# Two hybrid blocks on one core: the router on rows that are not yet normalised, the w_ada products in pairs, the attention's filling spread, and the order of the last experts

## The chip, the cores and the metric

The kernel runs on one core of one Trainium2 chip. The metric is device microseconds of one execution; the time before is 1055.93 us, the median of three runs (1053.69 to 1056.76).

## The reference, cut to what matters

256 rows of width 1024, float32, go through two blocks.

The first block: `h = rms_norm(x, g_mix)`, a projection by `w_in`, two attentions (8 causal heads with a forget gate, then 4 differential heads), gates, `w_o` and the residual. Then a mixture of experts:

```python
h = rms_norm(x, g_moe)
gl = h @ w_group + b_group            # 4 groups; the best one is taken
el = (h @ w_expert)[group] + b_expert # 8 experts of that group
ep = softmax(el); vals, idx = top_k(ep, 2); vals = vals / sum(vals)
weight = softmax(gl)[group] * vals
out[token] += weight * ((silu(h @ w1[e]) * (h @ w3[e])) @ w2[e])
x = rms_norm(x + out, g_final)
```

There are 32 experts; each has 6 MiB of weights (w1, w3: 1024x512, w2: 512x1024), all of which are read. The second block has `mod = silu(c) @ w_ada + b_ada` (w_ada is 1024x3072, 12 MiB, and depends on nothing computed before it), a projection by 1024x10240 weights, block attention, a short convolution, gates and output products.

## The kernel before, in words

Every engine runs a list of its own, in its order; semaphores join them. `O1.steps` (first block up to w_o) and `O2.steps` (second block) are lists of steps written out by a planner, and each engine's program walks them and does its share of each step.

**Weights.** SP loads chunks of 2 MiB in the order of the list `chunks` (line 831 issues each, the `dma_start` itself is L830). A chunk goes to a slot of a ring of five; the experts use three (areas 5, 6 and 7) besides, so eight chunks can be on their way or waiting. Four of six `ada` chunks stand behind `wo1` in the list; of those, the first has an area of its own (slot 8). SP waits in order: a chunk is issued when the one before it in its slot is used up (`released`). The first expert chunks wait for `s_y` 4 (the input of w_o is complete), the one in area 7 for the end of w_o.

**Products.** The dense products run on fp32r pairs: ACT copies a quarter chunk to its rounded high part (L1835), DVE or POOL subtracts to get the low part (L1253, L2187), and PE makes three products. All `matmul` calls go through L778. The experts use plain float32 weights.

**The attention's filling.** From the projections dq on, the dense products are handed out by a generator, `fill_first`: in each of 18 iterations of the attention loop, `next(fill)` is called twice (for i below 16), and puts one quarter chunk (or one w_ada product) between the small steps of a head: scores (`qk`), bias (`bf`), softmax (`soft` on DVE and ACT), transposes (`p_turn`, L965), P times V. The generator has 30 pieces, five are taken ahead of the loop; what is left at i = 16 is run then. `pa`, `pb` (the outputs of both attentions times w_pa, w_pb), then `wo0`, `wo1` follow.

**w_ada.** `ada_pe(i)`: eight products of a 32-column stationary (silu(c), divided by 32, in each column) with 512 columns of w_ada, into four groups of 32 partitions; ACT copies the bank to ACC; `ada_sum_pe(i)` adds the partitions by four one-column products with a column of ones. i = 0, 1 are run in the filling, i = 2 to 5 in the router.

**The router** (`route_pe` and `route` of each engine), after `wo1`: sum of squares per row on ACT (rows 0 to 127) and DVE (the others), rsqrt on POOL (L2175), scaled rows XS in the order of the experts' weights, 16 transposes (L959), 8 copies that multiply by g_moe, 8 products with the routing weights `wr`, transposes back, bias; then a chain of small DVE operations: softmax over groups, best group, softmax over its 8 experts, the two best, a table of selected experts SS. PE counts ranks by prefix sums (`cnt`), DVE builds PmR, the 0/1 matrix that selects the rows of four experts at a time (64 slots for each). XShR and XSlR are the high and low part of XS.

**The experts** (`experts_pe`). Per expert e: half a of w1, w3 (a chunk) times the gathered rows xe, `down(e-1)` (w2 of the expert before), every second time `scatter` (two experts added back to their rows, with PTR, into four accumulating banks), half b, two `gather` steps for the group of four that comes next (row selection by PmR, evicted by DVE with the factor g_moe), and two transposes of the activation Hb (L1202). ACT does Silu (L2011), copies y out (L1990) and makes its high part with the expert's weight as factor (L2000); DVE multiplies, evicts, and makes the low part. For e >= 28 DVE also makes four diagonals (L1256), PE spreads them over the partitions (8 matmul records) and DVE copies the result (L1622), as `spread`. At k = 1 of each four, PE multiplies PmR with the weights W32, which gives the weight of each slot. After the last expert each engine tests whether an expert has more than 64 rows (`flag`), which these inputs don't give; PE does so behind the last scatter, then runs five warm-up products, and goes on to the second block, whose first work on PE is `turn3` (transposes, L959).

## Time and profile before

| | us |
|---|---|
| median of 3 runs | 1055.93 |
| profiled execution, its time | 1055.72 |
| profiled execution, its span | 1053.9 |
| PE busy | 989.2 (94%) |
| DVE, ACT, POOL busy | 393.3, 368.7, 125.2 |
| moved by DMA | 307.92 MB |

The span starts with the first instruction and ends with the last; the time of an execution holds 1.8 us more than the span. "PE" is the matrix engine's products, "PEld" its weight loads, "SPq" the queue on which SP issues DMAs. The clock column is the granted clock of PE as a share of full speed: 1.00 is 2.4 GHz, 0.50 is 1.2 GHz. A busy PE is one with a product under way, whatever its clock.

### The profile page before, as it was taken

What the parts mean: (1) busy time and instruction counts of PE and PEld (TensorE: products, weight loads), DVE (VectorE), ACT (ScalarE), POOL (GpSimd) and SP (SyncE); (2) the same over time, 40 slices, a digit from 0 to 9 for tenths busy, and PEclk for the clock granted to TensorE, in tenths of its full rate; (3) what the DMA queues carried; (4) which work ended last, traced back from release to release, by engine and by line L of the source; (5) the groups of instructions that cost most, each with busy time, mean ns of one, the idle gap of its engine ahead of it and who ended that gap; (6) DMA issues with size and microseconds to landing.
All of it is one profiled execution on the core that took longest, in us unless ns stands there. A gap on an engine that the chain in (4) does not pass through costs nothing.

```text
span 1053.9 us, 14601 instructions
## 1 busy us (share of the span) xinstructions
PE 989.2 (94%) x6197; PEld 690.7 (66%) x6197; DVE 393.3 (37%) x761; ACT 368.7 (35%) x606; POOL 125.2 (12%) x79
## 2 busy tenths in 40 slices
PE   7999997999999999999999898876999999999996
PEld 6888886965434443443333333336999999999994
DVE  4454446845111111121211111125334444774464
ACT  4546664541111111111111111115445555554443
POOL 1111020120000000000000000001321111351122
PEclk9999998998999999999999999996999999999998
DMA  8973644697999999999999999995555545445300
GB/s 277 382 263 143 239 162 161 225 421 300 412 420 419 420 419 419 419 419 420 419 420 419 420 419 420 418 401 215 179 212 187 187 141 187 161 160 195 145 2 40
DMA packets 84043, 307.92 MB, mean 292 GB/s; under 512 B 6623, under 2 KB 13176, under 8 KB 59392
## 3 DMA queue, kind: packets, MB, share of 16 engines
q1 hardware_dynamic: 80184, 302.16, 73.2%
q10 hardware_dynamic: 3784, 4.73, 1.4%
q8 instruction: 51, 0.84, 0.3%
q14 instruction: 24, 0.20, 0.1%
HBM read 305.81 MB, written 2.63 MB: 293 GB/s over the span
## 4 chain that ended last, share of the span: by engine, by line
PE 65%; SPq 17%; DVE 8%; ACT 4%; DMA 3%; issue 2%; POOL 1%; POOLq 0%; ACTq 0%; DVEq 0%
PE bank L778 63%; SPq L830 17%; DMA ring<-in_w 3%; DVE arena L1253 2%; DVE arena L1256 2%; DVE wR L1253 2%; DVE arena L1259 1%; ACT wR L1835 1%; PE bank L1202 1%; ACT arena L2011 1%; PE bank L965 1%; POOL small L2175 1%; POOL wR L2187 0%; DMA arena<-in_x 0%; PE bank L959 0%
## 5 line engine op out<-in xcount | busy, mean ns | idle before, releaser
L778 PE MATMUL bank<-hTR,wR 128*128 128x256 f32 x2520 | 316.2, 286 | 5.6 <-DVE hTR L1253 2.3
L778 PEld LDWEIGHTS bank<-hTR,wR 128*128 128x128 f32 x2520 | 307.9, 193 | 10.0 <-issue 5.1
L778 PE MATMUL bank<-ring,arena 128*64 128x512 f32 (+1 forms) x1040 | 224.8, 596 | 8.9 <-DMA ring<-in_w 8.0
L1835 ACT ACTIVATE wR<-ring 128x1024 fp32r<-128x1024 f32 x161 | 168.3, 1054 | 109.8 <-PE bank L778 108.0
L1253 DVE TENSOR_TENSOR wR<-ring,wR 128x1024 fp32r<-128x1024 f32 x125 | 155.3, 1247 | 136.1 <-ACT wR L1835 135.7
L778 PE MATMUL bank<-arena 128*64 128x512 f32 (+8 forms) x794 | 169.0, 535 | 6.3 <-DMA arena<-in_w 3.4
L778 PEld LDWEIGHTS bank<-ring,arena 128*64 128x64 f32 (+1 forms) x1040 | 68.7, 135 | 141.3 <-issue 128.8
L1253 DVE TENSOR_TENSOR arena<-arena,bank 128x256 f32<-128x256 f32 (+1 forms) x36 | 16.1, 450 | 349.1 <-ACT arena L2011 347.4
L1990 ACT ACTIVATE arena<-bank 64x512 f32<-64x512 f32 x64 | 37.9, 593 | 288.7 <-PE bank L778 288.4
L2187 POOL TENSOR_TENSOR wR<-ring,wR 128x1024 fp32r<-128x1024 f32 x36 | 87.9, 2440 | 331.3 <-ACT wR L1835 331.3
L778 PEld LDWEIGHTS bank<-arena 128*64 128x64 f32 (+5 forms) x794 | 65.2, 149 | 90.8 <-issue 83.4
L2175 POOL TENSOR_TENSOR small<-small,mhalf 128x1 f32<-128x1 f32 (+1 forms) x12 | 9.0, 756 | 490.4 <-DVE small L1259 482.9
L2011 ACT ACTIVATE arena<-bank 128x256 f32<-128x256 f32 x32 | 12.3, 384 | 106.5 <-PE bank L778 106.5
L778 PE MATMUL bank<-wR,hTR 128*128 128x512 f32 x192 | 45.3, 393 | 0.0
L778 PEld LDWEIGHTS bank<-PmR,XShR 128*128 128x128 f32 x128 | 25.1, 196 | 24.5 <-issue 23.5
L778 PEld LDWEIGHTS bank<-wR,hTR 128*128 128x128 f32 x192 | 35.6, 188 | 8.3 <-issue 1.0
L778 PE MATMUL bank<-PmR,XShR 128*128 128x256 f32 x128 | 36.4, 315 | 0.7 <-DVE small L1436 0.6
L778 PE MATMUL bank<-PmR,XSlR 128*128 128x256 f32 x128 | 33.0, 289 | 0.0
L1256 DVE TENSOR_SCALAR arena<-bank,col 128x256 f32<-128x256 f32 x68 | 30.0, 478 | 6.5 <-PE bank L778 5.7
L1253 DVE TENSOR_TENSOR arena<-bank,arena 128x512 f32<-128x512 f32 (+2 forms) x30 | 19.6, 665 | 19.3 <-PE bank L778 17.0
L778 PEld LDWEIGHTS bank<-PmR,XSlR 128*128 128x128 f32 x128 | 25.3, 198 | 0.0
L1253 DVE TENSOR_TENSOR arena<-arena 128x512 f32<-128x512 f32 (+7 forms) x38 | 21.2, 565 | 10.9 <-ACT arena L2123 9.8
(207 smaller groups left out, 811.6 us busy)
## 6 DMA issues: line engine op xcount, KB each, us to landing
ring<-in_w SPq DMA_DIRECT2D x120, 1024.0 KB, 25.8
arena<-in_w SPq DMA_DIRECT2D x72, 1024.0 KB, 25.5
ring<-in_w_in SPq DMA_DIRECT2D x29, 2048.0 KB, 9.0
ring<-in_w_ada SPq DMA_DIRECT2D x5, 2048.0 KB, 9.2
ring<-in_w_o SPq DMA_DIRECT2D x2, 2048.0 KB, 7.8
ring<-in_w_o_attn SPq DMA_DIRECT2D x2, 2048.0 KB, 7.8
ring<-in_w_o_conv SPq DMA_DIRECT2D x2, 2048.0 KB, 8.2
ring<-in_w_out SPq DMA_DIRECT2D x2, 2048.0 KB, 9.2
```

The costliest lines, as they stand in the source:

```text
L778: return pe.e.matmul(o, l, r, start=start, stop=stop)
L830: e.e.dma_start(to[:, at_:at_ + k * n].rearrange("p (k n) -> p k n", k=k), part).then_inc(landed[nm][0], 16)
L965: last = eng.transpose(banks[u.bank][:, 128 * c:128 * c + 128], P[:, 128 * c:128 * c + 128], ident[:, :])
L1202: last = eng.transpose(banks[x.bank][:, 128 * c:128 * c + 128], Hb[e % 2][:, c:256:2], ident[:, :])
L1253: return eng.tensor_tensor(o, a, b, op)
L1256: return eng.tensor_scalar(o, a, s1, s2, op0) if op1 is None else eng.tensor_scalar(o, a, s1, s2, op0, op1)
L1259: return eng.scalar_tensor_tensor(out=o, in0=a, scalar=s, in1=b, op0=op0, op1=op1)
L1835: eng.activation(h, w, ACT.Copy).then_inc(s_high, 1)
L1990: last = eng.activation(Y[h0:h0 + 64, 512 * h:512 * h + 512], banks[u.bank][64 * h:64 * h + 64, :], ACT.Copy)
L2011: eng.activation(Hb[e % 2], banks[u.bank][:, 0:256], ACT.Silu).then_inc(S["silu"], 1)
L2175: eng.tensor_tensor(o, a, mhalf[:, 0:a.shape[1]], ALU.pow).then_inc(after, 1)
L2187: eng.tensor_tensor(l, pieces[i][1], h.bitcast(F32), ALU.subtract).then_inc(low[i][0], 1)
```

## The change

1. *Router on unscaled rows.* The squares, transposes and logits are made from XN itself, the first 512 columns of it amid the products of `wo1` (steps `turn2`, `xsplit`, `logits`), the others after it. The routing weights are multiplied by g_moe once, beforehand. The logits come out with rows in partitions, and the row's factor rsqrt is applied there. The high and low parts are those of unscaled rows; the row's factor goes into Silu, into the multiplication behind it, and the expert's weight into the copy of y, by RW, which 16 small products make at k = 3 of each four (`slot_factors`; the first time in `gather(0, 7)`). Only what selects experts stays ahead of the first gather: no softmax over the 8 experts is made, and the weights (`weights`) follow behind the first four gathers.
2. *w_ada in pairs.* Two chunks go into one bank (column 1 and column 0 of each group of 32), with one copy and one sum of two columns. ada2 and ada3 move into the filling (before g2) and into the ring; ada4 and ada5 stay in the router; slot 8 goes.
3. *Even filling.* For i below 8 and even, the first `next(fill)` is left out; above, there are still two.
4. *Diagonals an expert ahead;* the spread bank is copied by ACT behind Silu.
5. *Last pair by halves:* ACT copies and rounds one half of the last y, then the other.
6. *PE's overflow test amid the experts:* after expert 15; experts 16 to 31 stand in both branches. Six warm-up products before the last scatter, 26 after it.

```diff
-        chunks += [gate[0], ada[0], gate[1], ada[1], gate[2], gate[3]]
+        chunks += [gate[0], ada[0], ada[1], gate[1], ada[2], ada[3], gate[2], gate[3]]
...
-        chunks += ada[2:]
-        slots += [RING + 3, free_next[0], free_next[1], free_next[2]]
+        chunks += ada[4:]
...
-            if i < 16:
+            if i > 7 or i % 2:
                 next(fill, None)
...
             for st in O1.chunk(f"wo{c}", uses, "y"):
                 O1.add(*st)
+                if c and st[3] == 0:
+                    for n in range(NT):
+                        PB.use(("hT2", 0, n), 2 + n)
+                    O1.add("turn2", 0)
+                elif c and st[3] == 1:
+                    O1.add("xsplit", 0)
+                elif c and st[3] == 2:
+                    PB.use("lg", 7)
+                    O1.add("logits", 0)
...
-            experts_pe(pe, eng, 0, PB, dict(zip(MOE_SEMS, [sem(n) for n in MOE_SEMS])))
+            experts_pe(pe, eng, 0, PB, S, 0, NE // 2)
             pe.wait_ge(s_flag, 1)
+            known = dict(pe.known)
             with eng.If(eng.value_load(flag[0:1, 0:1]) > SLOTS):
...
+            with eng.Else():
+                experts_pe(pe, eng, 0, PB, S, NE // 2, NE)
+                warm(pe, banks[7], 26)
             pe.known = known
-            warm(pe, banks[7], 5)
...
+            elif what == "logits":
+                c, u = a[0], U_["lg"]
...
+                    for j in range(4 * c, 4 * c + 4):
+                        last = mm(pe, banks[u.bank][:, 256 + 40 * n:292 + 40 * n], hT[:, j, 128 * n:128 * n + 128], wr[:, j, :],
+                                  j == 0 and n == 0, j == 7 and n == 1)
...
         def route_pe(pe, eng):
-            ada_pe(pe, 2)
-            ada_pe(pe, 3)
-            ada_sum_pe(pe, 2)
-            for j2 in range(4):
-                transposes_pe(pe, eng, U_["hT2", j2], XS, j2, (s_norm[0], 2), (s_norm[1], 2))
...
+            for m in (1, 0):
+                ada_pe(pe, 2, m)
...
+                if b == 0 and j == 7:
+                    last = slot_factors(0, banks[u.bank])
                 last.then_inc(u.full, 1)
+
+            def slot_factors(b, bank):
+
+                pe.wait_ge(s_weights, 1)
+                for i in range(EB):
+                    for n in range(NT):
+                        for h in range(2):
+                            last = mm(pe, bank[64 * h:64 * h + 64, 256 + 2 * i:258 + 2 * i],
+                                      PmR[:, b % 2, n, 64 * i:64 * i + 64].bitcast(F32), WR[:, n, EB * b + i, :], n == 0, n == 1)
+                return last
...
-                if k == 1:
-                    pe.wait_ge(s_w32, 1)
...
+                if k == 3 and b + 1 < NB:
+                    last = slot_factors(b + 1, banks[x.bank])
                 last.then_inc(x.full, 1)
...
-            down(NE - 1)
-            scatter(NE // 2 - 1)
+            if hi == NE:
+                down(NE - 1)
+                if r == 0:
+                    warm(pe, banks[6], 6)
+                scatter(NE // 2 - 1)
...
-                v.step(eng.tensor_reduce(em, ep8, AXX, ALU.max))
-                v.settle()
-                tt(ep8, ep8, bc(em, 8), ALU.subtract).then_inc(s_shift, 1)
...
+                v.wait_ge(s_xhigh, 4)
+                tt(by_eights(XSlR[:, 1, :], 1), in_order(XN[:, 1, :], 1), by_eights(XShR[:, 1, :], 1).bitcast(F32),
+                   ALU.subtract).then_inc(s_xlow_dve, 1)
...
+            def weights():
+                tt(ex5[:, :, 0:4], g8[:, :, 0:4], bc(two(gv8[:, :, 0:1]), 4), ALU.subtract)
+                tt(two(ex5[:, :, 4:5]), two(v8[:, :, 1:2]), two(v8[:, :, 0:1]), ALU.subtract).then_inc(s_shift, 1)
...
+                v.wait_ge(s_rexp, 1)
+                v.step(eng.tensor_reduce(gs, ex5[:, :, 0:4], AXX, ALU.add))
+                v.step(ts(den, two(ex5[:, :, 4:5]), 1.0, None, ALU.add))
...
+                tt(WR[:, :, :, 0], S01[0], S01[1], ALU.add).then_inc(s_weights, 1)
...
                 for j in range(4):
                     gathered(0, j)
+                if not r:
+                    weights()
...
-                    if r in (0, 3) and e >= 28:
-                        spread(e - 28, r, P, S)
...
+                    if r in (0, 3) and 27 <= e < NE - 1:
+                        diagonals(e - 27, r, P, S)
...
             def route():
...
+                for n in range(NT):
+                    x_high(1, n)
                 ada_rows(2)
...
+                    for h in range(2):
+                        cs = slice(512 * h, 512 * h + 512)
+                        eng.activation(Y[64:128, cs], banks[u.bank][64 * h:64 * h + 64, :], ACT.Copy,
+                                       scale=RW[64 * h:64 * h + 64, e // EB % 2, e % EB, 0:1]
+                                       ).then_inc(*((u.free, 1) if h else (S["yhalf"], 1)))
+                        if h:
+                            emptied(s, u)
+                        else:
+                            s.wait_ge(S["yhalf"], g + 1)
+                        eng.activation(YhR[q % 2][:, cs], Y[:, cs], ACT.Copy).then_inc(S["yhigh"], 1)
```

## Rows read from the trace of the kernel before

**Rows 1.** The page's chain of work that ended last, by engine.

```profile
PE 65%; SPq 17%; DVE 8%; ACT 4%; DMA 3%; issue 2%; POOL 1%; POOLq 0%; ACTq 0%; DVEq 0%
```

**Rows 2.** Windows: start:end, length, then PE, PEld, DVE, ACT, POOL busy, clock, DMA share, GB/s.

```profile
160.00:165.00 5.00, 4.44 (x38) 3.87 (x37) 3.72 (x16) 2.21 (x7) 0.00 (x0) 1.00 0.00 2
165.00:170.00 5.00, 1.76 (x14) 1.27 (x14) 2.34 (x10) 2.33 (x11) 0.90 (x2) 0.97 0.97 324
170.00:175.00 5.00, 2.55 (x9) 1.78 (x10) 3.95 (x19) 2.16 (x9) 0.00 (x0) 0.50 1.04 387
175.00:180.00 5.00, 5.00 (x26) 5.00 (x25) 2.48 (x10) 1.75 (x7) 0.89 (x2) 0.50 0.35 128
```

**Rows 3.** Timeline of PE, attention: start, length, engine, line, operation, shape, count.

```profile
114.36 1.92 PE L778 MATMUL bank<-ring,arena 128*32 128x512 f32 x16
...
175.32 5.17 PE L778 MATMUL bank<-oaR,wR 128*128 128x256 f32 x24
...
180.79 3.12 PE L778 MATMUL bank<-oaR,wR 128*128 128x256 f32 x24
```

**Rows 4.** Windows around the first experts and in their midst.

```profile
250.00:260.00 10.00, 9.90 (x48) 4.12 (x44) 2.33 (x6) 0.00 (x0) 0.00 (x0) 0.92 0.49 186
260.00:270.00 10.00, 9.81 (x50) 4.12 (x50) 1.63 (x4) 1.39 (x3) 0.00 (x0) 1.00 0.95 355
...
300.00:400.00 100.00, 98.44 (x500) 41.28 (x500) 21.02 (x48) 16.72 (x30) 0.00 (x0) 1.00 1.01 420
...
600.00:700.00 100.00, 90.04 (x450) 37.33 (x452) 17.07 (x43) 14.61 (x26) 0.00 (x0) 1.00 1.01 418
```

**Rows 5.** Timeline of SP's DMA issues; a chunk of an expert is x2.

```profile
207.46 2.09 SPq L830 DMA_DIRECT2D arena<-in_w  x4
...
228.01 12.99 SPq L830 DMA_DIRECT2D ring<-in_w  x6
254.07 6.85 SPq L830 DMA_DIRECT2D arena<-in_w  x4
```

**Rows 6.** Timeline of the router, from w_o's last residual add to the first gather.

```profile
224.42 0.69 DVE L1253 TENSOR_TENSOR arena<-bank,arena 128x512 f32<-128x512 f32 x1 [0.67 <-PE bank L778]
...
229.24 1.94 PE L959 MATMUL bank<-ident,arena 128*128 128x128 f32 x16 [0.31 <-ACT arena L1960]
...
237.87 0.24 DVE L1468 MAX8 arena<-arena 128x8 f32<-128x8 f32 x2
...
239.58 0.17 DVE L1484 TENSOR_REDUCE arena<-arena 128x2 f32<-128x16 f32 x1
...
240.65 0.17 DVE L1253 TENSOR_TENSOR arena<-arena 128x16 f32<-128x16 f32 x1
...
242.34 0.22 DVE L1253 TENSOR_TENSOR arena<-arena 128x64 f32<-128x64 f32 x1
...
245.44 0.58 PE L778 MATMUL bank<-PmR,XShR 128*128 128x256 f32 x1 [0.59 <-DVE small L1436]
```

**Rows 7.** Timeline of PE at k = 1: the eight products with W32.

```profile
437.60 0.63 PE L778 MATMUL bank<-arena,PmR 128*64 128x1 f32 x16
```

**Rows 8.** The group of expert-weight DMAs from 600 us on (nanoseconds; first and last start).

```profile
L830 SPq DMA_DIRECT2D ring<-in_w x20: 2141/2143/4097, 604.9 to 673.8; - x20
...
DMA to landing us min/median/max: 26.0/26.7/27.5
```

**Rows 9.** Timeline of PE at the last expert: the spread, then down(31).

```profile
702.34 1.16 PE L778 MATMUL bank<-arena,kpack 128*128 128x128 f32 x8 [1.72 <-DVE arena L1256]
...
704.66 3.65 PE L778 MATMUL bank<-ring,arena 128*64 128x512 f32 x16 [0.92 <-issue]
```

**Rows 10.** Timeline behind the last expert: ACT's first splits, PE's warm-up, then turn3.

```profile
710.82 2.94 ACT L1835 ACTIVATE wR<-ring 128x1024 fp32r<-128x1024 f32 x3
...
718.66 2.50 PE L778 MATMUL bank<-ident 128*128 128x128 f32 x10 [4.84 <-issue]
...
722.17 3.77 PE L959 MATMUL bank<-ident,arena 128*128 128x128 f32 x16 [1.01 <-ACT arena L2027]
```

More of the change, by code:

```diff
@@ L816, in released @@
             elif nm[:3] == "ada":
[L817 removed]
+                filled(e, U_["adaw", int(nm[3]) // 2])
             else:
@@ L1149, in scatter @@
                 last.then_inc(S["scat"], 1)
-            for j in range(4):
-                gather(0, j)
-            for e in range(NE):
+            if lo == 0:
+                for j in range(4):
+                    gather(0, j)
+            for e in range(lo, hi):
                 b, k = divmod(e, EB)
@@ L1462, in route @@
-                v.step(eng.memset(g8, NEG))
                 v.settle()
-                v.step(eng.tensor_copy(g8[:, :, 0:4], lg[:, :, 0:4]))
-                tt(ex4, lg[:, :, 0:4], bc(gm, 4), ALU.subtract).then_inc(s_shift, 1)
+                for n in range(NT):
+                    v.wait_ge(s_rs[n], 2)
+                    x, f = BL[:, 256 + 40 * n:292 + 40 * n], ss[:, 4 + n:5 + n]
+                    v.step(stt(g8[:, n, 0:4], x[:, 0:4], f, bias36[:, 0:4], ALU.mult, ALU.add))
+                    last = stt(lg[:, n, 4:36], x[:, 4:36], f, bias36[:, 4:36], ALU.mult, ALU.add)
@@ L1466, in route @@
+                last.then_inc(U_["lg"].free, 1)
                 v.settle()
@@ L1945, in first_steps @@
                         eng.dma_start(XN[:, n, :], x_d[128 * n:128 * n + 128, :]).then_inc(s_x2[n], 16)
-            def ada_rows(i):
-                u = U_["adaw", i]
+                elif what == "turn2":
+                    c = a[0]
+                    square(c, 0)
+                    u = U_["hT2", c, 0]
+                    filled(s, u)
+                    eng.activation(hT[:, 4 * c:4 * c + 4, 0:128], banks[u.bank][:, :].rearrange("p (j t) -> p j t", j=4),
+                                   ACT.Copy).then_inc(u.free, 1)
+                    square(c, 1)
+                elif what == "xsplit":
+                    for n in range(NT):
+                        x_high(0, n)
```

385 lines of the change are left out of this document (181 added, 204 removed).

## The prediction

> **What bounds the kernel now.** I read the chain of work that ended last first: PE carries 65% of it, SP's queue 17% [rows 1]. So the span is PE's work but for one stretch of about 179 us (17% of 1053.9) in which the experts' weights arrive too slowly. The windows show how the two meet [rows 4]: from 300 us on the DMAs move 420 GB/s without a pause while PE is busy 98.4 of 100 us; from 600 us on PE is busy only 90 of 100 us. PE starts the experts late, with the ring full, catches up, and then waits for weights. A product saved amid the experts is therefore worth nothing. Three things are worth time: an earlier first expert chunk, a pause of the DMAs that goes, and less work behind the last chunk.
>
> The pause is in the windows: 186 GB/s in 250 to 260 us and 355 in 260 to 270, against 420 [rows 4]. That is 10 x (420 - 186) / 420 = 5.6 us and 10 x (420 - 355) / 420 = 1.5 us, together 7.1 us. SP's timeline gives the reason [rows 5]: the chunks that fill the eight slots are issued between 207.46 and about 241 us, eight chunks of 2.1 MB at 420 GB/s last 5.0 us each, 40 us in all, and the next one is issued at 254.07, when the first half expert frees its slot. The router is too slow for the ring.
>
> Ahead of it, PE idles in the attention's last iterations, which have no filling left: 0.56 + 3.24 + 2.45 = 6.25 us in 160 to 175 us, and the clock is at 1.2 GHz from 170 to 180 us [rows 2].
>
> **The sum** is made against the profiled execution's own 1055.72 us (span 1053.9 and 1.8 around it); the median, 1055.93, stands 0.2 above, so I take the two as one. Two measurements of this kernel can be told apart from about 0.3%, 3.2 us.
>
> *Term A, filling and w_ada (up to the start of w_o).* Lost now: 6.25 us idle, and of the 7.55 us that PE is busy at half clock half would go, 3.8 us (the first 24 products of pa took 5.17 us, the next 3.12: 2.05 of it [rows 3]). Ten in all. In the new order the first four even iterations give up one piece each, and the filling has 32 pieces: 5 are taken ahead, 12 in iterations 0 to 7, the rest lasts to the middle of iteration 15. Five pieces of about 3.1 us go where PE now waits 6.25. Added: ada2 and ada3, 1.92 us each [rows 3], 3.84 us; the sums stay two, each now with two columns. So -10.0 + 3.8 = -6.2. The thinner early iterations leave PE some 6.4 us between a head's scores and its transposes' turn, where softmax needs about 5; I charge 1 us. **A = -5.2**, bounds -6.2 and +1 (the late idle is softmax latency that no filling covers, and w_ada costs something). It carries through: `s_y` 4, and with it the first expert chunk, moves from 207.46 to about 202.3.
>
> *Inside w_o* PE gets 8 transposes at 0.12 us (16 took 1.94 [rows 6]) and 8 products of a 128-column stationary in two passes, another 1.9 us: +2.9 us. The DMAs run meanwhile, so this costs nothing if the router stays short enough; without that cover, 2.9.
>
> *Term B, the router and the pause.* I count from w_o's last product, W, now about 224.4, then 224.4 - 5.2 + 2.9 = 222.1. Residual add 0.7 [rows 6], 8 transposes of which four wait for it, a copy of 512 columns 0.7, the last products with wr 1.0: logits at W + 3.2. The factor (ACT's square, POOL's power) comes at about W + 3. Four small additions 0.7. The DVE chain from the first MAX8 to the table SS took 242.56 - 237.87 = 4.7 us; softmax over the experts, 239.58 to 240.82, leaves it [rows 6]: 3.4. From SS to the first gather it took 2.9 us; fewer count products ahead, but the subtraction of the last low part sits there now: 2.7. First gather at W + 10, 232.1, against 245.44. First half expert done: four gathers and their eviction 2, 16 products 3.65 [rows 9]: W + 15.7 = 237.8, where the ring runs dry only at about 204 + 40 = 244 to 245. The second chunk is needed about 5 us later, and stands behind gathers 4 to 7 and `slot_factors`, which waits for DVE's `weights` (some 15 operations of 0.2 us and ACT's exponential): W + 24.2 = 246.3 against 248.4. So the pause goes, with 2 us to spare at its narrowest point. **B = -7.1**; bounds -7.1 and 0.
>
> *At nothing, and what hides it.* `slot_factors`: 16 products where k = 1 had 8 for 0.63 us [rows 7], so +0.6 us per four experts, under the weights' arrival. ada4, ada5 in the router: 3.84 us of PE between the logits and the counts, under DVE's chain. The issues of ada2 and ada3 move ahead on SP; g2 and g3 stand behind them and have two or three iterations to arrive. ada4 and ada5 stay ahead of the experts' chunks and are issued once g3 and pa are used up.
>
> *The test for overflow.* Behind PE's branch the trace shows 4.84 us until the next product, at half clock [rows 10]; they are hidden now by the second norm. Amid the experts they fall on PE where the weights set the pace: from 600 us on it has 8 us to spare in each 100 [rows 4]. So I take 0, and 4.8 if nothing covers it. The Trainium skill, "Runtime: NRT & Kernel Launch", section "Instruction fetch mechanics", speaks against this edit: a taken branch to a target outside the fetched window stalls until its code is there; the trace agrees that there is a stall, and by the rule it is paid in any place, so only cover decides.
>
> *Term C, behind the last weights.* The last DMA is issued at 673.8 and lands after 26.7: 700.5; the chunk before it, half b of expert 31 (e31b), lands 5 us earlier, 695.5 [rows 8]. down(31) starts at 704.66, 9.2 us later [rows 9], since PE comes late: in each of the last experts the spread (1.16 us) waits for Silu, multiplication and diagonals. With diagonals ready it runs under Silu and multiplication: 3.65 + 1.16 + transposes, copy and handing 0.9 = 5.7 us. **C = -3.5**, bounds -5 and -1 (the landing is known to 0.7 us).
>
> *Term D, the tail.* ACT's four copies and roundings take as long in either order, and its first split, at 710.82 [rows 10], stands behind them, with DVE's low part and the second norm behind that. So halves bring scatter forward by a microsecond but not the norm. Warm-ups keep PE at full clock: the 16 transposes took 3.77 us where the router's took 1.94 [rows 6, 10]; only the first four are in the chain: 0.5. **D = -0.6**, bounds -2 and +1. By "TensorE: Matmul & The Clock Gate", Part 4, in the Trainium skill, transposes don't count as activity for the clock; by that rule D would be 0, though the router's transposes did run at 2.4 GHz.
>
> The second block's order is unchanged. Sum: -5.2 - 7.1 - 3.5 - 0.6 = -16.4; 1055.7 - 16.4 = **1039.3 us**.
>
> **The rivals.**
> 1. *The attention's end can't be filled* (A at +1): softmax of the last heads, not PE, sets it. For: in 165 to 175 us DVE is busy 6.3 of 10 us, with two engines in turn. Against: in 160 to 165 us, with filling, PE hardly waits. 1039.3 + 6.2 = 1045.5.
> 2. *The pause stays in part:* the second chunk's slot comes free late, since gather 7 waits for the weights of the slots. For: 2 us to spare, over ten estimated steps. Each microsecond beyond costs one; all of it gives 1039.3 + 7.1 = 1046.4.
> 3. *The change hardly does what it says:* both of the above; only C and D are left, 1055.7 - 4.1 = 1051.6.
> 4. *Slower: the branch amid the experts.* PE jumps over 16 experts and three more rounds of 32 while the DMAs are saturated. If the fetch took S us instead of 4.84, it would use up the slack first (8 us per 100 over the last 15 experts, 225 us: 18 us, [rows 4]); slower than before by 0.3% needs S > 18 + 16.4 + 3.2 = 38 us. Against: the same kind of jump took 4.84 with the same queues full [rows 10]. At S = 40 the time is about 1061. That is also the form in which the skill's rule would decide.
>
> **How the numbers follow.** Forecast, 1036 to 1043: 0.64. Better than 1034 (A at its bound, C and D too): 0.05. Rival 1: 0.12. Rival 2: 0.11, between 1040 and 1047. Rival 3: 0.05. Rival 4: 0.03. The range takes the forecast and rivals 1 and 2: 1034 to 1047. Faster by over 0.3%: all but rival 4 and half of rival 3, 0.94; within 0.3%: 0.03; slower: 0.03.
>
> **What would show it.** A: no idle and full clock on PE from 160 to 180 us, first expert chunk issued near 202. B: no window below 415 GB/s between the first expert chunk and the last, first gather near 232. The branch: a gap of about 5 us on PE near expert 16 and no DMA pause with it. C: down(31) 5.7 us after e31b's landing, near 688. D: turn3 some 14 us behind down(31), transposes at full clock. Wrong would be: a window with little DMA traffic around 245 to 255 us, PE late behind landed chunks at expert 31, or new idle on PE in the early attention.

## The result, and the profile after

Four executions of the changed kernel had a median of 1043.54 us (1041.2 to 1044.56), four of the kernel before 1055.31; the ratio is 0.9886, with a 95% interval of 0.987 to 0.9901. A repetition later gave 1043.22 against 1054.78 and 0.9895 (0.9882 to 0.9909). The change is faster by 11.6 to 11.8 us; forecast were 16.4 (1039.3 us) with a range of 1034 to 1047. The profiled execution took 1041.2 us (span 1039.4) and was the fastest of its four.

The page's chain of work that ended last, by engine, in the changed kernel:

```profile
PE 76%; DVE 9%; ACT 4%; SPq 4%; DMA 3%; issue 2%; POOL 1%; POOLq 0%; DVEq 0%; ACTq 0%
```

SP's queue had 17% of the chain [rows 1], now 4%: the weights set the pace for a far shorter stretch. Windows of the changed kernel, with the columns of [rows 2] and [rows 4]:

```profile
160.00:165.00 5.00, 5.00 (x44) 4.54 (x44) 4.89 (x12) 0.96 (x2) 2.37 (x1) 1.00 0.46 171
165.00:170.00 5.00, 5.00 (x45) 5.00 (x44) 3.02 (x9) 3.98 (x9) 0.00 (x0) 1.00 0.04 2
170.00:175.00 5.00, 5.00 (x44) 5.00 (x44) 2.35 (x9) 3.38 (x12) 0.88 (x2) 1.00 0.98 349
175.00:180.00 5.00, 2.96 (x19) 2.72 (x18) 4.62 (x11) 2.36 (x3) 0.00 (x0) 0.82 0.20 71
180.00:185.00 5.00, 5.00 (x39) 5.00 (x38) 1.92 (x2) 3.85 (x11) 0.81 (x2) 0.84 0.08 9
...
250.00:255.00 5.00, 4.66 (x26) 2.37 (x26) 1.69 (x4) 0.47 (x1) 0.00 (x0) 1.00 1.00 411
255.00:260.00 5.00, 5.00 (x26) 1.72 (x24) 0.00 (x0) 0.86 (x2) 0.00 (x0) 1.00 1.01 405
260.00:270.00 10.00, 9.65 (x48) 3.82 (x46) 1.70 (x4) 0.98 (x2) 0.00 (x0) 1.00 1.01 423
460.00:465.00 5.00, 0.00 (x0) 0.00 (x0) 0.98 (x4) 0.00 (x0) 0.00 (x0) 0.65 1.01 411
465.00:470.00 5.00, 4.11 (x10) 1.24 (x12) 0.00 (x0) 0.00 (x0) 0.00 (x0) 0.50 1.00 416
470.00:475.00 5.00, 5.00 (x22) 1.60 (x20) 0.00 (x0) 0.00 (x0) 0.00 (x0) 0.83 1.02 421
600.00:700.00 100.00, 94.47 (x477) 40.55 (x475) 18.19 (x47) 21.52 (x36) 0.00 (x0) 1.00 1.02 416
```

Three things are to be seen. The pause of the DMAs is gone but for a rest: 405 to 423 GB/s from 250 to 270 us. The prediction's mark, no window below 415, is missed by the 411 and 405 here and by 400 GB/s in 225 to 230 us; against 420 the three come to 0.5 us. The waits in the attention are filled up to 175 us, but a new one stands in 175 to 180 us, with a lower clock in it and behind it. And at 460 to 470 us PE stands still beside DMAs at full rate: the jump amid the experts.

The timeline of PE at the attention's end, at the jump, and from the last expert on, in the changed kernel (start, length, engine, line, operation, shape, count, idle time ahead in brackets, and what ended it):

```profile
172.46 3.05 PE L778 MATMUL bank<-oaR,wR 128*128 128x256 f32 x24
...
177.76 0.56 PE L972 MATMUL bank<-ident,arena 128*128 128x128 f32 x3 [2.04 <-DVE arena L1284]
178.07 4.62 PE L778 MATMUL bank<-oaR,wR 128*128 128x256 f32 x24
...
458.67 1.10 PE L778 MATMUL bank<-arena,PmR 128*64 128x2 f32 x32
465.89 6.53 PE L778 MATMUL bank<-ring,arena 128*64 128x512 f32 x16 [6.13 <-issue]
...
680.26 3.65 PE L778 MATMUL bank<-ring,arena 128*64 128x512 f32 x16 [0.43 <-DMA ring<-in_w]
...
685.89 3.65 PE L778 MATMUL bank<-ring,arena 128*64 128x512 f32 x16
689.48 1.16 PE L778 MATMUL bank<-arena,kpack 128*128 128x128 f32 x8
...
691.71 3.65 PE L778 MATMUL bank<-ring,arena 128*64 128x512 f32 x16 [0.56 <-issue]
```

The first block of the output product behind the stall takes 4.62 us where the one ahead of it took 3.05. The spread of expert 31 (1.16) now stands directly behind the last second product, with no wait, where it had 1.72 [rows 9]; down(31) starts 5.8 us behind the start of that product. SP's timeline in the changed kernel:

```profile
205.70 2.04 SPq L834 DMA_DIRECT2D arena<-in_w  x4
...
226.24 7.81 SPq L834 DMA_DIRECT2D ring<-in_w  x6
243.13 7.78 SPq L834 DMA_DIRECT2D arena<-in_w  x4
```

The first expert chunk came 1.8 us earlier (207.46 in [rows 5]), where 5.2 were forecast; the first one that needs a freed slot 10.9 us earlier (254.07).

Two instants of each profile split its span into three parts, and nearly all readings below rest on them: the issue of the first expert chunk on SP, and the start of down(31) on PE. All in us; times are medians.

| kernel | first chunk issued | from there to down(31) | from down(31) to the span's end | time |
|---|---|---|---|---|
| before | 207.46 | 497.2 | 349.2 | 1055.3 |
| after | 205.70 | 486.0 | 347.7 | 1043.5 |
| after, again (e12) | 207.53 | 486.2 | 347.7 | 1043.2 |
| e1 filling as before | 212.53 | 486.0 | 347.4 | 1048.5 |
| e2 PE's test last | 208.60 | 485.8 | 348.6 | 1043.8 |
| e3 ACT's test amid too | 208.69 | 486.6 | 347.0 | 1043.2 |
| e4 router late | 207.60 | 498.6 | 347.6 | 1054.6 |
| e5 rows padded | 206.19 | 486.1 | 347.8 | 1041.9 |
| e6 filling to the end | 206.59 | 486.0 | 346.2 | 1041.0 |
| e7 before, even filling | 204.96 | 497.3 | 347.9 | 1052.1 |
| e8 diagonals late | 205.09 | 494.1 | 348.9 | 1050.3 |
| e9 e8 and e2 together | 206.89 | 490.2 | 347.8 | 1047.0 |
| e10 combined | 202.71 | 485.9 | 345.0 | 1038.1 |
| e11 before, 113 rows | 210.31 | 495.8 | 346.9 | 1055.4 |

The middle part is the steadiest: the eight kernels that have the change's router and its early diagonals, and no delay put in (after, e12, e1, e2, e3, e5, e6, e10), lie between 485.8 and 486.6. The three that have the old router and no such delay (before, e7, e11) lie between 495.8 and 497.3. The first part scatters by 3.6 us between kernels whose code up to there is the same (after, e2, e3, e4, e8, e9, e12: 205.09 to 208.69, median 207.53), the last by about 2. So a first part is compared with that spread in mind. Part of it is the granted clock: the first 192 products of the projection take 23.3 us in some profiles, 24.8 in others of the same code, and 26.0 in e7, whose clock is 0.66 in 14 to 24 us (0.98 in the changed kernel).

### The profile page after: what moved, and what is told of

Same layout as the page of the kernel before. It is cut to its first block, busy times and chain, and to the rows that moved or that the text cites. A ratio compares the mean times of both kernels' runs of the same rounds, so it can differ in the third digit from the quotient of the medians.

```text
span 1039.4 us, 14926 instructions
## 1 busy us (share of the span) xinstructions
PE 993.1 (96%) x6369; PEld 698.2 (67%) x6369; DVE 391.2 (38%) x749; ACT 375.6 (36%) x611; POOL 123.7 (12%) x82
## 4 chain that ended last, share of the span: by engine, by line
PE 76%; DVE 9%; ACT 4%; SPq 4%; DMA 3%; issue 2%; POOL 1%; POOLq 0%; DVEq 0%; ACTq 0%
PE bank L778 74%; SPq L834 4%; DMA ring<-in_w 3%; DVE arena L1284 3%; DVE arena L1281 2%; DVE wR L1278 2%; DVE arena L1278 1%; ACT arena L2028 1%; PE bank L1231 1%; ACT wR L1851 1%; DMA arena<-in_rows 1%; PE bank L972 1%; POOL wR L2222 1%; ACT arena L1913 0%; DVE small L1281 0%
## 5 line engine op out<-in xcount | busy, mean ns | idle before, releaser
L778 PE MATMUL bank<-ring,arena 128*64 128x512 f32 (+2 forms) x1056 | 228.6, 602 | 8.4 <-issue 6.7
L778 PE MATMUL bank<-arena 128*64 128x512 f32 (+7 forms) x778 | 164.5, 529 | 0.7 <-DVE small L1410 0.7
L778 PEld LDWEIGHTS bank<-ring,arena 128*64 128x64 f32 (+2 forms) x1056 | 70.1, 136 | 141.2 <-issue 137.4
L1284 DVE SCALAR_TENSOR_TENSOR arena<-bank,small,arena 128x256 f32<-128x256 f32 x32 | 15.5, 484 | 346.3 <-ACT arena L2028 346.3
L1999 ACT ACTIVATE arena<-bank,small 64x512 f32<-64x512 f32 x62 | 42.3, 683 | 280.6 <-PE bank L778 280.3
L778 PEld LDWEIGHTS bank<-arena 128*64 128x64 f32 (+4 forms) x778 | 63.5, 148 | 83.7 <-issue 77.1
L2028 ACT ACTIVATE arena<-bank,small 128x256 f32<-128x256 f32 x32 | 15.2, 474 | 82.1 <-PE bank L778 82.1
L1913 ACT ACTIVATE arena<-arena,small 128x128 f32<-128x128 f32 (+1 forms) x32 | 14.3, 448 | 29.7 <-DVE small L1281 29.7
## 6 DMA issues: line engine op xcount, KB each, us to landing
ring<-in_w_o SPq DMA_DIRECT2D x2, 2048.0 KB, 11.6
```

Of the source, the lines that this page charges most:

```text
L778: return pe.e.matmul(o, l, r, start=start, stop=stop)
L1284: return eng.scalar_tensor_tensor(out=o, in0=a, scalar=s, in1=b, op0=op0, op1=op1)
L1913: last = eng.activation(P[:, x:y], P[:, x:y], ACT.Exp, bias=st[:, 2 + n:3 + n], accum_out=st[:, 4 + n:5 + n])
L1999: last = eng.activation(Y[h0:h0 + 64, 512 * h:512 * h + 512], banks[u.bank][64 * h:64 * h + 64, :], ACT.Copy, scale=RW[64 * h:64 * h + 64, ...
L2028: eng.activation(Hb[e % 2], banks[u.bank][:, 0:256], ACT.Silu, scale=RW[:, e // EB % 2, e % EB, 1:2]).then_inc(S["silu"], 1)
```

## The experiments

**e1, the filling as before, all else changed.**

```diff
-            if i > 7 or i % 2:
+            if i < 16:
```

> The changed kernel with the filling handed out as before (two pieces in every iteration below 16); all else as changed. The profile of the changed kernel shows PE idle for 2.04 us at 175.7 to 177.8 and at less than full clock for the next 24 products of pa (4.62 us in place of 3.12), so the first expert chunk is issued only 1.8 us earlier than before (205.70 against 207.46). Theory 1 (the thinning is worth what it moves under the last heads, and its shortfall is the last head's own softmax): without it, the 32 pieces end in iteration 13, PE idles some 3 to 4 us in all in iterations 14 to 16, and the clock falls; first expert chunk issued at 207 to 209, time 1.5 to 3.5 us above the changed kernel, 1043 to 1046 us. Rival (the two added w_ada products fill the gap by themselves, and thinning is worth nothing, since the chain of DVE and ACT sets the end): first expert chunk at 205.0 to 206.5, time as the changed kernel within 0.8 us.

Measured: 1048.53 us (1046.78 to 1050.16), ratio 0.994 (0.9928 to 0.9952). The attention's end on PE in e1's timeline:

```profile
174.59 0.44 PE L1059 MATMUL bank<-ident,arena 128*128 128x128 f32 x2 [1.48 <-DVE arena L1281]
177.50 0.90 PE L972 MATMUL bank<-ident,arena 128*128 128x128 f32 x3 [2.46 <-DVE arena L1284]
179.74 1.62 PE L778 MATMUL bank<-arena 128*128 128x128 f32 x6 [1.34 <-ACT arena L1928]
```

Three waits of 5.3 us in all stand where the changed kernel has one of 2.04, and the time is 5 us longer, with the first chunk at 212.53. Theory 1 is right in its direction and too low in its size (207 to 209 and 1.5 to 3.5 us were expected); the rival is out. Without the even filling nothing would be left of term A; it pays for the two moved w_ada products too.

**e7, the kernel before with that condition alone.**

```diff
-            if i < 16:
+            if i > 7 or i % 2:
```

> The kernel before with one condition changed: the filling of the attention is held back in every second of its first eight steps, as in the changed kernel; nothing else of the change. Theory 1: the even filling is worth about 5 us in the changed kernel, where the rest had put more work in front (less filling is left for the end); in the kernel before, whose waits at the end sum to less, it gives 2 to 4.5 us: 1050.5 to 1053. Rival, my own first reckoning turned round: the filling of the kernel before is short as a whole, so holding it back moves the waits to the front and gives under 1 us: 1054 to 1055.5.

Measured: 1052.06 us (1049.68 to 1052.41), ratio 0.9962 (0.995 to 0.9975): 3.5 us below the 1055.53 of the kernel before in the runs beside it. The attention's own stretch can be measured from the block of 24 products that waits for POOL's split, just ahead of it. In the kernel before:

```profile
59.44 3.11 PE L778 MATMUL bank<-hTR,wR 128*128 128x256 f32 x24 [0.72 <-POOL wR L2187]
```

and in the changed kernel:

```profile
60.47 3.10 PE L778 MATMUL bank<-hTR,wR 128*128 128x256 f32 x24 [0.71 <-POOL wR L2222]
```

From there to the first chunk's issue it took 142.9 us in e7 (62.07 to 204.96), before 148.0 (59.44 to 207.46), in the changed kernel 145.2 (60.47 to 205.70), in e1 149.7 (62.85 to 212.53). So even filling gives 5.1 there in the kernel before and 4.5 in the changed one, and the rest of the change takes 2.3 back. That these are the two w_ada products in it (1.92 us each [rows 3]), less what they cover, is a reckoning; they were not run apart.

**e6, the filling thinned out to step 10.**

```diff
-            if i > 7 or i % 2:
+            if i > 10 or i % 2:
```

> The changed kernel with the filling of the attention spread thinner at its beginning (every second step up to step 10 instead of 7), so that its last piece falls beside the last head. Theory 1: the 2.0 us in which TensorE waits for the last head, and the half clock after it (first block of the output product at 4.62 us instead of about 3.1), are uncovered because the filling is used up one to two steps too soon; then the idle time at the end is under 0.7 us, the clock stays full there, and the time falls by 2 to 4 us against the changed kernel: 1040 to 1042. Rival: the first steps now lack filling, so that the waits return there in the same amount; then the wait at the end goes and others of 0.5 to 1 us each appear before 110 us, and the time is 1042.5 to 1045.

Measured: 1040.95 us (1039.02 to 1041.32), ratio 0.9857 (0.9843 to 0.9872). All of PE's waits from 66 to 205 us in e6's timeline:

```profile
76.54 1.12 PE L778 MATMUL bank<-arena 8*128 8x256 f32 x4 [0.73 <-DVE small L1410]
186.90 0.44 PE L1059 MATMUL bank<-ident,arena 128*128 128x128 f32 x2 [0.31 <-DVE arena L1281]
```

The wait of 2.04 us is gone, no other came early (the changed kernel has the wait of 0.73 too), the granted clock is 1.00 in 170 to 190 us, and the way from that block of 24 products to the first chunk is 143.5 us (63.14 to 206.59). In it the 48 products behind the wait of 0.73 took 7.50 us, at a clock of 0.83 in 75 to 85 us; in e10, which has the same filling, they took 6.02, and the way is 142.0 (60.73 to 202.71). The wait at the end was a filling used up too soon, and could have been covered.

**e5, the packed rows padded from 113 to 128 with zeros.**

```diff
-NROW = 113
+NROW = 128
...
+    arrays["rows"] = np.concatenate(rows + [np.zeros((NROW - sum(len(r) for r in rows), 128), rows[0].dtype)])
```

> The changed kernel with the packed parameter rows filled up from 113 to 128 rows with zeros (one transfer of 64 KB instead of 56.5, and a transpose of 128 rows). Theory 1: 113 is a prime number of rows, so the transfer is not shared out evenly over the DMA engines and holds up the queue behind it; with 128 rows TensorE's first transpose waits at most 1 us for the rows instead of 2.6 to 3.1, its first product starts 1 to 2.5 us earlier than in the changed kernel (15.7 in its profile, 16.6 to 17.2 in two others of the same early code), so at 14.0 to 15.2, and the time is 1041 to 1043. Rival: the eight more rows only cost their bytes, or the late start is scatter between executions; then the first product still starts at 15.7 to 17.2, and the time is 1043 to 1044.5.

Measured: 1041.9 us (1041.37 to 1042.82), ratio 0.9872 (0.9857 to 0.9886). PE's first transpose in the changed kernel, from PE's timeline:

```profile
9.52 0.32 PE L893 MATMUL bank<-ident,arena 113*128 113x113 f32 x1 [2.63 <-DMA arena<-in_rows]
```

and SP's issues of the rows and of the two weight pieces behind them, the same kernel:

```profile
2.11 0.33 SPq L845 DMA_DIRECT2D arena<-in_rows  x1
2.48 4.83 SPq L847 DMA_DIRECT2D ring<-in_w_in  x2
```

The same two views of e5, PE's first:

```profile
6.72 0.42 PE L893 MATMUL bank<-ident,arena 128*128 128x128 f32 x1
```

and SP's:

```profile
2.11 0.43 SPq L845 DMA_DIRECT2D arena<-in_rows  x1
2.58 1.06 SPq L847 DMA_DIRECT2D ring<-in_w_in  x2
```

With more bytes the transfer is ready at least 2.8 us earlier (no wait for it is left), and the two issues behind it take 1.06 us in place of 4.83. The first product starts at 14.16 instead of 15.73. By the medians the time is 1.3 to 1.6 us shorter; the intervals overlap, so that much isn't shown.

**e11, the kernel before with its 105 rows padded to 113.**

```diff
-NROW = 105
+NROW = 113
...
+    arrays["rows"] = np.concatenate(rows + [np.zeros((NROW - sum(len(r) for r in rows), 128), rows[0].dtype)])
```

> The kernel before with its 105 packed rows filled up with zeros to 113, nothing else. Theory 1: 113 rows, a prime number, are not shared out over the DMA engines; TensorE's first transpose then waits 2 us and more for them instead of 0.6, the queue behind them is late too, and the first product starts at 15.5 to 17.2 instead of 14.6 to 14.7; the time is 1056 to 1058. Rival: the number of rows is nothing, and the late start came from something else in the changed kernel; then the first product starts at 14.6 to 14.8 and the time is 1055 to 1056.

Measured: 1055.41 us (1054.27 to 1060.83), ratio 1.0011 (0.9999 to 1.0023). PE's first transpose in e11:

```profile
9.71 0.32 PE L891 MATMUL bank<-ident,arena 113*128 113x113 f32 x1 [2.92 <-DMA arena<-in_rows]
```

and SP's two issues behind the rows:

```profile
2.48 5.18 SPq L843 DMA_DIRECT2D ring<-in_w_in  x2
```

The start is late here too (first product at 16.75; 14.70 before), so the number of rows does it. The time moved by 0.6 us, inside its interval, under the 1 to 3 that I had expected: the late start is real, what it costs at the end isn't settled. Whether it is that 113 is prime was not tried apart: only 105, 113 and 128 ran.

**e4, the router held up:** 48 more of the 128-column warm-up products ahead of the first gather.

```diff
+                if r == 0:
+                    may_write(pe, P.of["g", r, 0, 0])
+                    warm(pe, banks[P.of["g", r, 0, 0].bank], 48)
```

> The changed kernel with 48 warm-up products on PE ahead of the first gather, some 12 us: it puts the first gather back from 235.9 to about 248, near where it was before the change (245.4). Theory 1 (the first experts' gain is the DMA pause alone, up to what the ring covers): the DMAs stand still between about 247 and 254 us; windows below 415 GB/s there add up to 5 to 9 us lost, the last chunk lands by that much later, and the time is 5 to 9 us above the changed kernel, less than the 12 us of delay, as PE has reserve for the rest. Rival (the arrival is set elsewhere, and the pause is made up for): time less than 2 us above the changed kernel. Rival 2 (PE, not DMA, sets the experts' length since its test and factors were added): the time rises by the whole 12 us.

Measured: 1054.62 us (1053.03 to 1055.65), ratio 0.9997 (0.9988 to 1.0007). Windows of e4:

```profile
245.00:250.00 5.00, 5.00 (x47) 5.00 (x47) 0.00 (x0) 0.00 (x0) 0.00 (x0) 1.00 0.85 354
250.00:255.00 5.00, 4.90 (x39) 3.99 (x39) 2.61 (x12) 0.21 (x1) 0.00 (x0) 1.00 0.01 5
255.00:260.00 5.00, 4.89 (x33) 2.74 (x30) 3.12 (x11) 0.00 (x0) 0.00 (x0) 1.00 0.32 72
260.00:265.00 5.00, 5.00 (x53) 2.48 (x52) 0.56 (x2) 1.76 (x2) 0.00 (x0) 1.00 0.83 351
265.00:270.00 5.00, 4.65 (x25) 2.04 (x26) 1.69 (x4) 0.00 (x0) 0.00 (x0) 1.00 0.91 334
```

The first gather came 13.8 us later, measured from the first chunk's issue (43.96 against 30.16); the delay was larger than I had meant. The middle part grew by 12.6 us (498.6 against 486.0), the time by 11.1. Theory 1 has the cause: against 420 GB/s the five windows lose 66 + 415 + 348 + 69 + 86 GB/s over 5 us each, 11.7 us in all. Its size, 5 to 9 us, was too low. Rival 2's size fits as well, but not its cause: at the last two experts PE still waits for weights (1.34 and 0.38 us), so they set the pace. If each microsecond of the router beyond the reserve costs one, the reserve is 1.2 us, where the forecast had 2; a single delay can't show that it is one for one.

**e8, the diagonals of the last four experts in their own expert again.**

```diff
-                    if r in (0, 3) and 27 <= e < NE - 1:
-                        diagonals(e - 27, r, P, S)
...
+                    if r in (0, 3) and e >= 28:
+                        diagonals(e - 28, r, P, S)
```

> The changed kernel with the diagonal matrices of the last four experts made in their own expert again, as before, instead of one expert ahead; the last pair by halves and everything else as changed. Theory 1: the spread of the last expert's weights waited in the kernel before only because it stood behind its diagonals, a chain of 1 to 3 us between the last expert's second product and the down product; so the down product of the last expert starts 7 to 9 us after that second product instead of 5.8, and the time is 1044.5 to 1046.5. Rival: the diagonals were ready in time anyway and only the halves of the last pair shorten the end; then the distance stays at 5.8 and the time at 1043 to 1044.

Measured: 1050.31 us (1047.18 to 1053.28), ratio 0.995 (0.9933 to 0.9967). PE's waits at the last four experts in e8's timeline:

```profile
647.32 1.16 PE L778 MATMUL bank<-arena,kpack 128*128 128x128 f32 x8 [1.87 <-DVE arena L1281]
...
665.01 1.38 PE L778 MATMUL bank<-arena,kpack 128*128 128x128 f32 x8 [1.97 <-DVE arena L1281]
...
680.41 1.13 PE L778 MATMUL bank<-arena,kpack 128*128 128x128 f32 x8 [1.97 <-DVE arena L1281]
...
697.26 1.16 PE L778 MATMUL bank<-arena,kpack 128*128 128x128 f32 x8 [1.88 <-DVE arena L1281]
```

The last distance is as expected (7.5 us from the last second product to down(31)), but the price is four times that: 1.87 + 1.97 + 1.97 + 1.88 = 7.7 us, and the middle part grew by 8.1. Both of my theories had looked at the last wait alone. That 7.7 and 8.1 are so near is in part chance. The changed kernel's waits for weights in this stretch (1.30 and 0.43 us) are gone here, which gives 1.7 back. And the clock fell behind two of the waits (0.79 in 650 to 655 us, 0.66 in 665 to 670): 32 products took 8.78 us that take 7.09 in the changed kernel, and 16 took 4.83 for 3.65, 2.9 more. That makes 7.7 - 1.7 + 2.9 = 8.9, which fits the 8.1 to within the 0.8 us by which this distance scatters.

**e2, PE's test behind all 32 experts, the rest changed.**

```diff
-            experts_pe(pe, eng, 0, PB, S, 0, NE // 2)
+            experts_pe(pe, eng, 0, PB, S, 0, NE)
...
-            with eng.Else():
-                experts_pe(pe, eng, 0, PB, S, NE // 2, NE)
-                warm(pe, banks[7], 26)
...
+            warm(pe, banks[7], 5)
```

> The changed kernel with PE's overflow test back behind the last scatter, and five warm-up products behind it in place of 26 (the six before the last scatter stay); all else as changed. In the changed kernel PE stands still for 6.13 us behind its branch at expert 16, the DMAs move 420 GB/s throughout, and PE does not wait for weights again before 614 us (445 before). Theory 1 (the stall is hidden in both places): down of the last expert starts within 0.3 us of the changed kernel's 691.7, the gap of 5 us and more comes back between the last scatter and the warm-ups, turn3's first transposes run at half clock, and the second block starts 0.3 to 1.0 us later: time 0.3 to 1.0 us above the changed kernel. PE then waits for weights from about 500 us on. Rival (the stall costs PE its reserve at the end): down of the last expert starts over 1 us earlier, time 1 us or more below the changed kernel.

Measured: 1043.76 us (1042.11 to 1044.82), ratio 0.989 (0.9875 to 0.9904): the same as the change. The middle part is 485.8; behind the last expert e2 shows

```profile
709.82 2.50 PE L778 MATMUL bank<-ident 128*128 128x128 f32 x10 [5.66 <-issue]
712.11 3.10 PE L962 MATMUL bank<-ident,arena 128*128 128x128 f32 x16
```

The stall is hidden in either place; the tail is 0.6 us longer (turn3 17.7 us behind down(31), 17.1 in the changed kernel), which is theory 1. The rival is out: down(31) didn't come over 1 us earlier behind the first chunk.

**e9, e8 and e2 together.**

> The changed kernel with the diagonals of the last four experts in their own expert and, with them, TensorE's test for overflow behind all 32 experts again. Alone, late diagonals lengthened the way from the first expert chunk's issue to the last down product from 486.0 to 494.1 us (time 1050.3), and the test behind the experts alone left it at 485.8. Theory 1: both draw on one reserve, the time by which TensorE is ahead of the weights; the jump amid the experts (6.1 us of idle time and a stretch at half clock) uses it up, and the diagonals ahead (four waits of 1.9 us saved) pay for it. Without the jump the late diagonals cost less: the way is 488 to 491 us and the time 1045.5 to 1048. Rival: the two are independent, the late diagonals cost 8 us wherever the test stands; then the way is 493 to 495 us and the time 1049.5 to 1051.5.

Measured: 1047.04 us (1046.56 to 1052.38), ratio 0.9933 (0.9916 to 0.9951), middle part 490.2. Both are in theory 1's ranges and outside the rival's: the two draw on one reserve. The late diagonals cost 490.2 - 485.8 = 4.4 us without the jump and 494.1 - 486.0 = 8.1 with it; the jump costs 0.2 with early diagonals and 3.9 with late ones. These are differences of one profile each, of a distance that repeats to 0.8 us; the times of e8 and e9 alone, whose intervals overlap, would not show it. PE's waits for weights from 250 us on are the reserve: 8.5 us in e2, 5.3 in e9, 1.7 in the changed kernel, none in e8.

**e3, ACT's experts 16 to 31 behind its own branch as well.**

```diff
-            def experts(r, P, S):
+            def experts(r, P, S, lo=0, hi=NE):
...
-                for e in range(NE):
+                for e in range(lo, hi):
...
-            finish = experts(0, PB, dict(zip(MOE_SEMS, [sem(n) for n in MOE_SEMS])))
+            S0 = dict(zip(MOE_SEMS, [sem(n) for n in MOE_SEMS]))
+            experts(0, PB, S0, 0, NE // 2)
...
-                finish()
+                experts(0, PB, S0, NE // 2, NE)()
```

> The changed kernel with ACT's overflow test moved amid the experts as well: experts 16 to 31 and the last pair in both branches of ACT's program. In the changed kernel ACT tests after its last spread copy (ends 691.27) and its next instruction starts only at 696.57, 5.30 us later, while the bank it copies was full at 695.36: 1.2 us in the chain that ends last. Before the change ACT reached its test at 701.0 and was needed at 708.35, 7.3 us later, so the same fetch was hidden. Theory 1 (the shorter way to the last product laid ACT's instruction fetch bare): ACT's first copy of the last y starts within 0.1 us of the end of down, the second block starts 1.0 to 1.4 us earlier, time 1.0 to 1.4 us below the changed kernel. Rival (ACT is held by something else at that point, or the norm behind waits for DVE anyway, whose own gap of 1.65 us comes back once it arrives earlier): the copy starts earlier and the second block does not; time unchanged or up to 0.5 us below.

Measured: 1043.18 us (1041.1 to 1044.13), ratio 0.9883 (0.9868 to 0.9897). ACT's first operation behind down(31), in the changed kernel:

```profile
696.57 0.68 ACT L2041 ACTIVATE arena<-bank,small 64x512 f32<-64x512 f32 x1 [5.30 <-issue]
```

and in e3:

```profile
699.01 0.68 ACT L2041 ACTIVATE arena<-bank,small 64x512 f32<-64x512 f32 x1 [4.14 <-PE bank L778]
```

In the changed kernel ACT came 4.86 us behind down(31)'s start, though the product had ended at 695.36, 1.2 us ahead, and the trace shows nothing that it waited for. In e3, with the branch elsewhere, it is 3.69: the wait is the branch's. With that, turn3 follows down(31) by 15.9 us in place of 17.1. The trace gains 1.2; the median, 0.4, can't confirm it.

**e12, the change again.**

> The changed kernel once more, on the chip of the runs beside it, as the measure for differences of one to three microseconds: 1042.5 to 1044.5. Its profile also tells whether the early start seen in its first profile (first expert chunk issued at 205.7) or the later one of its variants (207.6 to 208.7) is the usual one; I expect 206.5 to 208.5.

Measured: 1043.22 us (1042.78 to 1046.04), and a first chunk at 207.53. The first profile's early start (205.70) was a favourable one.

**e10, e3, e5 and e6 together.**

> The changed kernel with three edits together: the packed rows filled up to 128, the filling spread to step 10 of the attention, and ScalarE's half of the experts behind its own branch too. If they add up (the rows 1.6 us by median, the filling 2.6, ScalarE's branch 1.2 in its trace and 0.4 by median), the time is 1038 to 1040.5. Rival: the gains of the first two are one and the same, since each only changes how much filling is left for the last heads; then it is 1040.5 to 1041.5.

Measured: 1038.06 us (1035.41 to 1038.99), ratio 0.9837 (0.9824 to 0.9849), which lies clear of the change's 0.9882 to 0.9909. It is 5.2 us below the change run beside it, where the three gains alone sum to 4.6 by their medians, and 16.7 below the kernel before. The gains add up: the first chunk goes out at 202.71, and turn3 comes 15.9 us behind down(31).

## Why the forecast held, and where it fell short

**Term A failed in its size.** Its step "Ten in all. ... Five pieces of about 3.1 us go where PE now waits 6.25" took the whole late idle time as fillable by this edit. The filling ended one head too soon: 2.04 us of idle time stayed, and with it the clock at 0.82 and 0.84 in 175 to 185 us, 1.5 us more on the next block of products (4.62 us for 3.12). On the attention's own stretch the gain was 148.0 - 145.2 = 2.8 us, where 5.2 were forecast. With the filling to the end it is 4.5 in e6 and 6.0 in e10, so the size was within reach, with the filling spread further. The bound in the prediction, softmax latency that no filling covers, is refuted by e6.

The other half of the miss was in no step: the prediction has no term for the packed rows, which grow from 105 to 113, 4 KB more. PE's first transpose waited 2.6 to 3.4 us in the profiles with 113 rows (0.62 before), and the first product starts 1.0 to 2.5 us late (15.73 to 17.24, median 17.06 of the seven profiles of the same early code, for 14.70). That eats up most of the 2.8 us: the first chunk comes at 207.5 in the median of the seven, where it came at 207.46 in the only one of the kernel before. As a result A is close to 0 in the typical run, 1.8 in the profiled one. How much of the late start reaches the end isn't settled: e5 and e11 move the time by less than their scatter. For the thinner early iterations 1 us was charged; there is one wait of 0.73 us at 73.9, and in e4, e5 and e12 the clock fell behind it, which cost 1.5 us there.

**Term B held.** The first gather came at 235.86; forecast was 232.1, and 3.4 of the difference is A's shortfall, so the ten estimated steps of the router were off by 0.4 together. The pause went but for 0.5 us. Its price is the middle part of e9 against the kernel before, 490.2 against 497.2: 7.0, forecast 7.1; against the other two kernels with the old router it is 5.6 (e11) and 7.1 (e7). Rival 2 was as close as it looked, with a reserve of about 1.2 us.

**Term C held, for a wider reason.** Forecast were 3.5 us from one wait at the last expert, with the landing as the floor. e9 against e2 gives 4.4. From the last second product to down(31) it took 5.8 us, as forecast (5.7). But the diagonals count at all of the last four experts: from 650 us on the changed kernel waits for weights only 1.30 and 0.43 us, so nearly every other wait there is paid for. In the prediction's own terms, e31b landed at 695.0 before (its second half, issued at 668.9, took 26.1 us) and at 685.1 in the changed kernel (659.1 and 26.0). From the first chunk's issue that is 487.5 and 479.4 us, 8.1 less, and from this landing to down(31) it is 9.7 and 6.6 us, 3.1 less. So the weights came earlier by more than the 7.1 of term B, and PE followed at 6.6 us where term C supposed 5.7; which of the two terms gets how much depends on how they are parted. The sum read from the windows began at 250 us and left out 235 to 245, with 365 and 392 GB/s, another 1.0 us.

**The jump** was hidden, as forecast, but was dearer than the 4.84 us that it was given: 6.13 us of idle time, and 6.53 us for products that take 3.65 at full clock, 9.0 us in all. "I take 0" was right only because term C stood beside it. The cover was read as 8 us in each 100 from 600 us on; of PE's idle time there, 5.4 us were waits for diagonals and only 4.3 waits for weights. With late diagonals the real cover was the 5.3 us of waits for weights in e9, and the jump cost 3.9. The Trainium skill, "Runtime: NRT & Kernel Launch", section "Instruction fetch mechanics", has a taken branch whose target isn't in the fetched window wait until its code is there. The traces agree that there is a stall behind these branches, both behind the experts and amid them, 4.3 to 6.3 us on PE and 5.3 to 6.2 on ACT; that it is the fetch they don't show.

**Term D held in sum, -0.6 forecast.** turn3 follows down(31) by 17.1 us instead of 17.5, and the long run of products behind it came a further 0.25 earlier. The reckoning by which D is 0, since transposes leave the clock low, did not come true: behind the warm-up products turn3's 16 transposes took 2.49 us for 3.77, at a clock of 1.00 in 705 to 710 us. The steps inside were others than I wrote: ACT's own stall, hidden before (it idled 7.30 us until the bank was full), was laid bare for 1.2 us. The changed kernel has ACT copy the spread bank behind Silu, so that it reaches its branch 1.3 us later behind Silu's start, and down(31) starts 1.9 us earlier behind it. Neither was undone alone; nor were the halves and the warm-up products, so what each of them gives isn't shown.

**The sum.** For the profiled executions: first part -1.8, middle part -11.2, last part -1.5, together the -14.5 between their spans, 1053.9 and 1039.4. In the repetition: +0.1, -11.0 and -1.6, together -12.5 (span 1041.4). The last part scatters by as much as D's size between kernels that are alike behind down(31), so only the distance to turn3 speaks for D. So the forecast gain was 4.6 to 4.8 us too large, by the 5.2 of term A less what the others gave above their forecast, and the range held because the other three terms did. Rival 1's number came half true, by a cause that isn't its own; rival 2 stayed out.

## What to carry to other kernels

Split each profile at two or three instants that every version has, and compare distances between them: here one such distance repeated to 0.8 us where whole times scatter by 3. Where two edits seem free or small by themselves, ask whether they draw on the same reserve; only the run with both undone tells. And read a change of a transfer's shape as a change of its time, even where its bytes hardly grow.

## What was not expected of the hardware

A transfer of 113 rows of 512 B held up PE by 2.6 to 3.4 us and lengthened the two issues behind it on SP's queue from 1.03 and 1.06 us (105 and 128 rows) to 4.83 and 5.18. An idle time of 2 us on PE was followed by products 1.5 times as long (4.62 us for 3.05, at a clock of 0.82 and 0.84). But the same idle time left the clock at its full level in other profiles, of kernels with the same attention: in e12, e4 and e5 it fell behind the wait of 0.73 us a hundred microseconds earlier instead (7.50 to 7.52 us for 6.02), and in e8 behind neither. So one profile can't price a short wait: these cost their length, and either 1.5 us more or nothing. ACT's copies out of a bank became dearer by the per-partition factor that they now apply; the page's costliest groups of the kernel before

```profile
L1990 ACT ACTIVATE arena<-bank 64x512 f32<-64x512 f32 x64 | 37.9, 593 | 288.7 <-PE bank L778 288.4
```

and of the changed one

```profile
L1999 ACT ACTIVATE arena<-bank,small 64x512 f32<-64x512 f32 x62 | 42.3, 683 | 280.6 <-PE bank L778 280.3
```

show 593 and 683 ns each; ACT has room for it, as the idle time behind the bar says.
